# A two-layer hybrid decoder trunk with a dense and a fetched path for its experts: 40 tokens instead of 32 on the fetched path, and expert activations rounded in pairs

## The reference

```
q  = h @ wq                                  # 8 heads x 256
s1, s2 = q[:half] @ k1, q[half:] @ k2        # 128 scores each
top 16 of each, top 16 of their 256 sums     # 8 x 16 = 128 picks for each token
gates = softmax(top scores)
act = gelu(sum_d h[t, d] * u[expert, d])     # one number for each pick
y[t] = sum_k act[t, k] * gate[t, k] * v[expert, :]
```

## Time and profile before

| | |
|---|---|
| median of 3 runs | 2004.48 us |
| span of the profiled execution, first to last instruction | 2001.2 us |
| PE busy | 1945.8 us, 97% |
| DVE busy | 1710.9 us, 85% |
| ACT busy | 1240.9 us, 62% |
| POOL busy | 441.9 us, 22% |
| DMA, mean over the span | 240 GB/s |

### The profile page before, as it was taken

The page is one execution under the profiler, slowest core; times in us unless marked ns, Lnnn a source line. Parts: engine busy times, 40 slices in busy tenths (PEclk is TensorE's granted clock), DMA queues, the critical chain, the costliest instruction groups (busy, mean ns, idle before and its releaser), DMA issues.

```text
span 2001.2 us, 39536 instructions
## 1 busy us (share of the span) xinstructions
PE 1945.8 (97%) x14478; PEld 1854.1 (93%) x14478; DVE 1710.9 (85%) x3168; ACT 1240.9 (62%) x2387; POOL 441.9 (22%) x312
## 2 busy tenths in 40 slices
PE   6999999999999999999989998999999999999998
PEld 6899899999999999999978898999999999999997
DVE  7876988999799888888788878899988888888887
ACT  3478545666888655555555775566668885555554
POOL 0000000000556433344100000000016543443440
PEclk7999999999999999999999999999999999999999
DMA  8764755666666799988767557555665558999884
GB/s 334 276 238 149 262 191 171 200 199 203 212 214 208 251 319 324 321 322 322 257 229 249 206 173 248 197 190 197 200 210 169 165 163 289 323 319 321 323 321 139
DMA packets 133554, 480.52 MB, mean 240 GB/s; under 512 B 16048, under 2 KB 16688, under 8 KB 132784
## 3 DMA queue, kind: packets, MB, share of 16 engines
q1 hardware_dynamic: 114992, 411.74, 60.6%
q0 software_dynamic: 18432, 67.12, 8.9%
HBM read 473.61 MB, written 1.57 MB: 237 GB/s over the span
## 4 chain that ended last, share of the span: by engine, by line
PE 87%; DVE 6%; ACT 3%; issue 2%; DMA 2%; SPq 0%; POOL 0%; DVEq 0%; ACTq 0%
PE ps L1777 20%; PE ps L1773 12%; PE ps L1474 11%; PE ps L1416 9%; PE ps L1412 8%; PE ps L1413 8%; PE ps L1478 6%; PE ps L1409 2%; PE ps L1746 2%; PE ps L1518 2%; ACT w_hi L564 2%; DVE w_lo L865 1%; DMA raw<-in_win 1%; PE ps L1464 1%; PE ps L1705 1%
## 5 line engine op out<-in xcount | busy, mean ns | idle before, releaser
L865 DVE TENSOR_TENSOR w_lo<-raw,w_hi 128x1024 fp32r<-128x1024 f32 x664 | 812.0, 1223 | 164.3 <-ACT w_hi L564 161.6
L564 ACT CAST w_hi<-raw 128x1024 fp32r<-128x1024 f32 x664 | 695.1, 1047 | 395.7 <-PE ps L1416 204.5
L1777 PE MATMUL ps<-p_both,w_hi 128*128 128x448 f32 x1952 | 440.1, 367 | 1.0 <-DVE p_both L1255 1.0
L1412 PE MATMUL ps<-h_both,w_hi 128*128 128x224 f32 (+1 forms) x1640 | 393.9, 282 | 2.5 <-ACT big L569 1.2
L1413 PE MATMUL ps<-h_both,w_hi 128*128 128x224 f32 (+1 forms) x1640 | 386.4, 278 | 0.0
L1777 PEld LDWEIGHTS ps<-p_both,w_hi 128*128 128x128 f32 x1952 | 349.3, 189 | 24.5 <-issue 1.3
L540 POOL TENSOR_SCALAR hot<-con,rt 128x128 f32<-128x128 f32 x168 | 198.1, 1190 | 640.0 <-DVE neg L1330 528.4
L1412 PEld LDWEIGHTS ps<-h_both,w_hi 128*128 128x128 f32 x1640 | 314.1, 192 | 5.5 <-issue 3.3
L1413 PEld LDWEIGHTS ps<-h_both,w_hi 128*128 128x128 f32 x1640 | 314.6, 192 | 0.0
L792 ACT CAST p_both<-big 128x224 fp32r (+1 forms) x256 | 97.0, 380 | 303.5 <-PE ps L1773 303.5
L1773 PEld LDWEIGHTS ps<-p_both,w_lo 128*128 128x128 f32 x2048 | 269.2, 191 | 7.6
(11 more groups left out here) (214 smaller groups left out, 2363.9 us busy)
## 6 DMA issues: line engine op xcount, KB each, us to landing
raw<-in_u SPq DMA_DIRECT2D x256, 512.0 KB, 3.5
raw<-in_v SPq DMA_DIRECT2D x256, 512.0 KB, 5.5
raw<-in_win SPq DMA_DIRECT2D x104, 512.0 KB, 4.4
hot<-in_ada SPq DMA_DIRECT2D x60, 512.0 KB, 4.9
big<-in_ada SPq DMA_DIRECT2D x36, 512.0 KB, 6.3
raw<-in_wq SPq DMA_DIRECT2D x32, 512.0 KB, 4.6
raw<-in_wout SPq DMA_DIRECT2D x16, 512.0 KB, 4.0
big<-in_decay SPq DMA_DIRECT2D x2, 1536.0 KB, 12.6
```

The costliest lines, as they stand in the source:

```text
L564: nc.scalar.copy(w_hi[:, j % 2, :], raw[:, j, :]).then_inc(hi_ready, 1)
L865: tt(w_lo[:, j % 2, :], raw[:, j, :], w_hi[:, j % 2, :].bitcast(F32), ALU.subtract).then_inc(lo_ready, 1)
L1412: mm(o, w, h_hi[:, k, 0:nd], start=(k == 0), stop=False)
L1777: return mm(bank(YC[c])[:, 0:2 * nd].rearrange("p (a t) -> p a t", a=2), w_hi[:, s, P * c:P * (c + 1)], p_both[:, s, :, 0:nd], start=begin ...
```

## The change

It sends 40 instead of 32 tokens through the fetched path and 216 instead of 224 through the dense one.

- `DENSE` falls to 216: matmuls of 448 columns get 432, those of 224 get 216. `N_GATE` falls from 28 to 27.
- `SP_GROUPS` is 3, on 120 partitions (`SP_ROWS`). `SP_STEPS` rises from 32 to 43, since 128 picks in three groups take 43 steps; the 129th pick has a weight of zero. There are 86 indirect DMAs of 120 rows for each layer instead of 64 of 128 rows. `dot_at` and `mix_at` spread 43 steps over the same 57 blocks. Since 86 is no multiple of four, slot numbers run on from layer to layer.
- The token rows of the last 40 tokens are copied by three DMAs from a buffer of their own (`h_own`), and three DMAs of 40 rows spread the picks instead of four of 32. ACT and DVE write the upper 64 partitions (`TAIL`) where they wrote 32.
- Activations are rounded two blocks at a time: one ACT copy of 2 x 216 and one DVE subtraction of 2 x 216 for blocks m and m+1. Two pair slots are needed; the second lies in `h_both`, which is free in the V stage. ACT's copy for blocks m+2 and m+3 waits for block m-1 instead of block m, and DVE's subtraction now stands behind the `w_lo` of block m+1 instead of ahead of it. PE waits for it at even blocks only.
- POOL's one-hot loop goes by single builds instead of pairs, as 27 is odd.

The diff, cut to its core:

```diff
-N_SPARSE = 32
+N_SPARSE = 40
...
-SP_STEPS = N_PICK // SP_GROUPS
+SP_STEPS = -(-N_PICK // SP_GROUPS)
+SP_PICKS = SP_GROUPS * SP_STEPS
+SP_ROWS = SP_GROUPS * N_SPARSE
+TAIL = slice(P // 2, P)
...
-        mixed = words(0, D)
-        h_tok = words(W_SCORE, D)
+        mixed = words(0, D)[0:SP_ROWS]
+        h_tok = words(W_SCORE, D)[0:SP_ROWS]
+        h_own = words(W_SCORE + 3 * D, D)
...
-                        for g in range(SP_GROUPS - 1):
-                            sp.dma_start(h_tok[N_SPARSE * g:N_SPARSE * (g + 1), :], h_tok[P - N_SPARSE:P, :]).then_inc(tok_spread, 16)
+                        for g in range(SP_GROUPS):
+                            sp.dma_start(h_tok[N_SPARSE * g:N_SPARSE * (g + 1), :], h_own[P - N_SPARSE:P, :]).then_inc(tok_spread, 16)
...
+                    slot = (2 * SP_STEPS * l + j) % SP_SLOTS
...
-                        rows_in[j % SP_SLOTS], None, u_flat if j < SP_STEPS else v_flat,
-                        bass.IndirectOffsetOnAxis(spread[:, 0, k:k + 1].bitcast(U32), 0)).then_inc(row_in[j % SP_SLOTS], 16)
+                        rows_in[slot], None, u_flat if j < SP_STEPS else v_flat,
+                        bass.IndirectOffsetOnAxis(spread[:, 0, k:k + 1].bitcast(U32), 0)).then_inc(row_in[slot], 16)
...
-                def round_p(m, s):
...
-                    nc.scalar.copy(p_hi[:, s, 0:nd], acts[:, ds(m, 1), 0:nd].rearrange("p a t -> p (a t)")
-                                   ).then_inc(phi_ready, 1)
+                def round_pair(m, s):
...
+                    nc.scalar.copy(pair_hi[s][:, 0:2, 0:nd], acts[:, ds(m, 2), 0:nd]).then_inc(phi_ready, 1)
...
-                        for s in range(2):
-                            round_p(s, s)
+                        round_pair(0, 0)
...
-                        if not (end and j >= 2):
-                            act.wait_ge(block_done, n + 1)
-                            round_p(m + 2, j % 2)
+                        if j % 2 == 0 and not (end and j):
+                            act.wait_ge(block_done, n)
+                            round_pair(m + 2, 1 - j // 2)
...
-                def low_p(m, s):
...
-                    dve.wait_ge(phi_ready, l * N_V + m + 1)
-                    tt(p_lo[:, s, 0:nd], acts[:, ds(m, 1), 0:nd].rearrange("p a t -> p (a t)"),
-                       p_hi[:, s, 0:nd].bitcast(F32), ALU.subtract).then_inc(plo_ready, 1)
+                def low_pair(m):
...
+                    s = m // 2 % 2
+                    dve.wait_ge(phi_ready, (l * N_V + m) // 2 + 1)
+                    tt(pair_lo[s][:, 0:2, 0:nd], acts[:, m:m + 2, 0:nd], pair_hi[s][:, 0:2, 0:nd].bitcast(F32), ALU.subtract
+                       ).then_inc(plo_ready, 1)
...
-                    dve.wait_ge(row_in[n % SP_SLOTS], 16 * (2 * SP_STEPS // SP_SLOTS * l + n // SP_SLOTS + 1))
-                    return rows_in[n % SP_SLOTS]
+                    slot, turn = (2 * SP_STEPS * l + n) % SP_SLOTS, (2 * SP_STEPS * l + n) // SP_SLOTS
+                    dve.wait_ge(row_in[slot], 16 * (turn + 1))
+                    return rows_in[slot]
...
-                        dve.wait_ge(tok_spread, 16 * (SP_GROUPS - 1) * (l + 1))
+                        dve.wait_ge(tok_spread, 16 * SP_GROUPS * (l + 1))
...
-                low_p(0, 0)
+                low_pair(0)
...
-                            low_p(RING * i + j + 1, (j + 1) % 2)
-                        if not (end and j == RING - 1):
...
+                        if j % 2 == 0 and not (end and j):
+                            low_pair(RING * i + j + 2)
...
-                def part_y(s, c, which):
-                    pp, vv = ((p_hi, w_hi), (p_lo, w_hi), (p_hi, w_lo))[which]
-                    return mm(bank(YC[c])[:, 0:nd], vv[:, s, P * c:P * (c + 1)], pp[:, s, 0:nd],
+                def part_y(j, c, which):
+                    pp, vv = ((pair_hi, w_hi), (pair_lo, w_hi), (pair_hi, w_lo))[which]
+                    return mm(bank(YC[c])[:, 0:nd], vv[:, j % 2, P * c:P * (c + 1)], pp[j // 2][:, j % 2, 0:nd],
...
-                def both_y(s, c, begin):
-                    return mm(bank(YC[c])[:, 0:2 * nd].rearrange("p (a t) -> p a t", a=2), w_hi[:, s, P * c:P * (c + 1)],
-                              p_both[:, s, :, 0:nd], start=begin, stop=False, skip_group_check=True)
+                def both_y(j, c, begin):
+                    return mm(bank(YC[c])[:, 0:2 * nd].rearrange("p (a t) -> p a t", a=2), w_hi[:, j % 2, P * c:P * (c + 1)],
+                              (h_both[:, :, j - 2, 0:nd] if j >= 2 else p_both[:, j, :, 0:nd]), start=begin, stop=False, skip_group_check=True)
...
-                        s = j % 2
...
-                        pe.wait_ge(plo_ready, l * N_V + m + 1)
+                        if j % 2 == 0:
+                            pe.wait_ge(plo_ready, l * (N_V // 2) + i * (RING // 2) + j // 2 + 1)
```

More of the change, by code:

```diff
@@ L242, in build @@
         p_hi, p_lo = p_both[:, :, 0], p_both[:, :, 1]
+        pair_hi, pair_lo = (p_hi, h_hi), (p_lo, h_lo)
         cond = sb("cond", [P, D])
@@ L261, in build @@
         cond_t = sb("cond_t", [P, KC])
-        spare = sb("spare", [P, 2 * N_PICK + 3 * SP_STEPS])
+        spare = sb("spare", [P, 2 * SP_PICKS + 3 * SP_STEPS])
         number16 = sb("number16", [P, TOPK], F16)
@@ L270, in build @@
         sel = con[:, K_SEL:K_SEL + N_SPARSE]
-        picked = spare[:, 0:2 * N_PICK].rearrange("p (a k) -> p a k", a=2)
-        spread = spare[:, 2 * N_PICK:2 * N_PICK + 2 * SP_STEPS].rearrange("p (a k) -> p a k", a=2)
-        dots = spare[:, 2 * N_PICK + 2 * SP_STEPS:]
+        picked = spare[:, 0:2 * SP_PICKS].rearrange("p (a k) -> p a k", a=2)
+        spread = spare[0:SP_ROWS, 2 * SP_PICKS:2 * SP_PICKS + 2 * SP_STEPS].rearrange("p (a k) -> p a k", a=2)
+        dots = spare[0:SP_ROWS, 2 * SP_PICKS + 2 * SP_STEPS:]
         def words(at, *shape):
@@ L308, in build @@
         acts = words(0, NKEYS, DENSE)
-        mixed = words(0, D)
-        h_tok = words(W_SCORE, D)
+        mixed = words(0, D)[0:SP_ROWS]
+        h_tok = words(W_SCORE, D)[0:SP_ROWS]
+        h_own = words(W_SCORE + 3 * D, D)
         mod_ring2 = words(W_SCORE + D, 2, D)
-        rows_in = [t[:].rearrange("p s b n -> p (s b n)")[:, D * a:D * (a + 1)] for t in (hot1, hot2) for a in range(2)]
+        rows_in = [t[:].rearrange("p s b n -> p (s b n)")[0:SP_ROWS, D * a:D * (a + 1)] for t in (hot1, hot2) for a in range(2)]
         u_flat = u_rows
@@ L531, in _, with hot @@
                 pool.wait_ge(gates_ready, l + 1)
-                def hot(i, first=False):
-                    for s in range(2):
[L535 to L544, removed]
+                def hot(b):
+                    if b >= 2:
+                        pool.wait_ge(gate_mat, N_GATE * l + b - 1)
+                    for t in range(POOL_TOK):
+                        col = ds(b * BATCH + t, 1)
+                        last = nc.gpsimd.tensor_scalar(hot2[:, b % 2, t, :], iota, rt[:, 1, col], rt[:, 2, col],
+                                                       ALU.is_equal, ALU.mult)
+                    last.then_inc(hot2_pool, 1)
+                for b in range(N_GATE):
+                    hot(b)
                 pool.wait_ge(picks_spread, 16 * SP_GROUPS * (l + 1))
@@ L829, in _ @@
                             act.wait_ge(score_used, l + 1)
-                        nc.scalar.copy(h_tok[P - N_SPARSE:P, 512 * half:512 * (half + 1)], bank(M[half])[P - N_SPARSE:P]).then_inc(tok_copied, 1)
+                        nc.scalar.copy(h_own[TAIL, 512 * half:512 * (half + 1)], bank(M[half])[TAIL]).then_inc(tok_copied, 1)
                     if 8 <= m < 8 + 4 * n_fill and m % 4 == 0:
@@ L901, in angle @@
                     dve.wait_ge(angles, 2 * a + 2)
+            nc.vector.memset(picked[TAIL, :, N_PICK:], 0.0)
             dve.wait_ge(sig_c, 1)
@@ L1250, in product @@
                     tt(acts[:, m, 0:nd], acts[:, m, 0:nd], acted[:, m % 2, 0:nd], ALU.mult).then_inc(producted, 1)
-                def low_p(m, s):
-                    dve.wait_ge(phi_ready, l * N_V + m + 1)
-                    tt(p_lo[:, s, 0:nd], acts[:, ds(m, 1), 0:nd].rearrange("p a t -> p (a t)"),
-                       p_hi[:, s, 0:nd].bitcast(F32), ALU.subtract).then_inc(plo_ready, 1)
+                def low_pair(m):
[3 more added lines that the diff above has]
+                       ).then_inc(plo_ready, 1)
                 def stage_picks():
-                    tail = slice(P - N_SPARSE, P)
-                    a1, a2, g = (res[tail, a, PH:2 * PH, :].rearrange("p h k -> p (h k)") for a in range(3))
-                    number, weight = picked[tail, 0, :], picked[tail, 1, :]
+                    a1, a2, g = (res[TAIL, a, PH:2 * PH, :].rearrange("p h k -> p (h k)") for a in range(3))
+                    number, weight = picked[TAIL, 0, 0:N_PICK], picked[TAIL, 1, 0:N_PICK]
                     us.done(stt(number, a2, float(NKEYS), a1, ALU.mult, ALU.add))
@@ L1795, in outputs_y @@
                                     if c not in held:
```

(13 more changed lines are left out.)

## The result

The changed kernel takes 2176.25 us (median of 5 runs, 2164.67 to 2180.98) against 2004.48 us (2002.85 to 2007.14): 1.085 times as long, 95% interval 1.083 to 1.087. The forecast was 1992, with a range of its own of 1984 to 1998. All of the loss arises in the two V stages: from ACT's copy of the last block of `u` to that of the last block of `v` it was 326.7 us in either layer, and it is 414.5 and 403.9 now.

What follows compares the result with a forecast made beforehand. PE, busy 97% of the span, was taken as the bound. Terms - 12.1 - 1.8 - 2.0 + 0.4 + 3.0 = - 12.5 us took the span from 2001.2 to 1988.7; plus 3.3 gave 1992.0 us, own range 1984 to 1998.

Steps and rivals of the forecast that it cites:

- Transfers, V stage: V stage: DMAs can supply 360 GB/s, loads landing in about 6.5 us; 3 us lost over both layers.
- The first rival: V stage: loads landing over about 7.5 us let the four-slot ring set the pace; 2023 us at 8 us; chance 0.21.
- the 3 us put down for late loads: V stage: some loads of over 8 us that PE feels, 3 us lost over both layers.
- Wide matmuls: V stage: 432 instead of 448 columns saves 6.2 ns in each of 1952 matmuls, 12.1 us (11.3 to 13.1).
- Narrow matmuls: Matmuls of 224 columns already lie on an f32 weight-load floor near 110 ns; 216 columns save nothing.
- Rounding in pairs: ACT's part off the path; DVE's first subtraction of each V stage 0.22 us longer, 0.4 us lost over both layers.
- the 0.4 of the sum: Start of the V stages: PE waits longer for DVE's first subtraction, 0.4 us lost over both layers (0 to 1).
- Wide matmuls, U stage: U stage: DVE's `w_lo` sets the pace from near block 29; PE gains 0.9 us a layer, 1.8 in all (0 to 6.4).
- Gate builds: One gate build fewer for each layer shortens PE's list by 0.98 us, 2.0 us in all (1.8 to 3.5).

Runs made afterwards that it cites:

- the nine phases without computation: Fetches and/or 512 KB weight loads only, all layer computation left out; beside loads, fetches of 128 rows moved 408 GB/s and of 120 rows 273.
- full fetches: Changed kernel, but each fetch fills all 128 partitions, rows 120 to 127 fetching unread row 0: 1985.53 us; repeated later, 1983.14 us.

## Why the prediction was wrong

By its own steps:

**Transfers, V stage: this step failed.** It said that the DMAs can do it, because they had moved 426 GB/s with four fetches queued. That row was of fetches of 128 rows; the change fetches 120. I counted the smaller fetch as 6% less traffic, and it lowers what all 16 DMA engines deliver, the untouched weight loads included, in the nine phases without computation from 408 to 273 GB/s, in the kernel to 266. The demand of 360 GB/s was then 30% too much. For 128 rows the step holds: with full fetches the same window moved 363 GB/s. The two pages of the Trainium skill named above describe ports and dealing; I had read "120 rows" as a size and not as a shape.

**The first rival had the right path and the wrong cause.** It said that late loads let the ring set the pace, (landing + 1.05 + 1.23 + 0.2) / 4 for a block. With the 10.9 us measured that is 3.35 us; blocks 2 to 61 of layer 0 took 192.3 / 59 = 3.26. The 2023 us of this rival are 153 us short of what came. But I let it begin from traffic and stop at a landing of 8 us, and gave it 0.21. With full fetches, where its conditions were met as I had meant them (12% more traffic, DVE at 94% of the window), it didn't occur: ACT waited for loads for 15.6 us in 12 blocks of layer 0 and PE 0.2 us for a `w_lo`. So the 3 us put down for late loads measure 0.4 over both layers when the fetches are full; DVE held, as forecast.

```profile
ACT w_hi L570 <- DMA raw<-in_v: 15.6, 12, 1.5
...
PE ps L1780 <- DVE w_lo L869: 0.2, 1, 0.2
```

**Wide matmuls: right, undersized.** 448 to 432 columns was to save 6.2 ns of 204. In the chain of the V stage with full fetches eight take 1.57 us, 196 ns, and eight narrow ones 0.88:

```profile
882.15 1.57 PE ps L1784 x8
883.72 0.88 PE ps L1780 x8
884.60 1.56 PE ps L1784 x8
```

That is 8 to 9 ns each, more than the 6.7 of 16 columns at 2.4 GHz, 16 to 17 us in all instead of 12.1. The slope between 448 and 512 columns wasn't the slope below 448.

**Narrow matmuls: right.** Still 0.88 / 8 = 110 ns; 216 columns gain nothing. The page is read too narrowly in the prediction: the section that it cites of the Trainium skill ("TensorE: Matmul & The Clock Gate", Back-to-back issue gap) gives N / 2.4 + 2.5 ns for an isolated matmul, and says that in a stream of weight loads and matmuls both set the spacing. This kernel is such a stream, so the 111 ns don't contradict it.

**Rounding in pairs: right.** PE's waits for the first subtraction of a V stage rose from 1.0 to 1.4 us over both layers, the 0.4 of the sum.

**Wide matmuls, U stage: right.** For block 60 of layer 0 `w_lo` ends at 466.67 + 1.21 = 467.88 and PE's narrow part starts at 467.93, a lead of 0.05 us where it was 0.79. First DVE, then PE of the changed kernel:

```profile
466.67 1.21 DVE L867 TENSOR_TENSOR w_lo<-raw,w_hi 128x1024 fp32r<-128x1024 f32 x1
...
467.93 1.15 PE L1482 MATMUL ps<-h_both,w_lo 128*128 128x216 f32 x8
```

The lead reached this 0.05 us at block 29, the block that the prediction named, and from there two of every five blocks have no more (it said every fifth). Up to block 30 the stage was 1.5 us shorter than before; up to block 71 it is 0.8 us shorter in layer 0 and 1.1 in layer 1, for 0.9 forecast, since DVE sets the pace in between.

**Gate builds: right in sign, the size uncertain.** Blocks 71 to 127 of layer 1 take 180.5 to 180.6 instead of 181.0 us, those of layer 0 between 1.9 and 0.2 us less in the four profiles with 27 builds. Over both layers that is 0.7 to 2.3 us, where 2.0 was forecast (1.8 to 3.5).

**What the forecast would have been without the failed step.** For the version with full fetches, the last one profiled, the distances between ACT's copies of the same weight blocks in the two traces give:

```
us, both layers       before   pairs, full fetches   change   forecast
U stage, 0 to 127      750.5         747.0            -3.5      -3.8
V stage, to 127        653.3         637.2           -16.1      -8.7
```

The V row runs from the last block of U to the last of V. Its forecast is -12.1 + 0.4 + 3.0: its two errors, 4 to 5 us too little for the matmuls and 3 us for late loads that didn't show, have the same sign. With full fetches the kernel measured 1985.53 and 1983.14 us, 6 and 9 us under the forecast of 1992, the second just below its range.

## What to carry to other kernels

A DMA's destination is a shape and not a number of bytes: before giving up partitions of a transfer, measure it alone with the new number of rows, and keep the full 128 with dummy rows if it slows. Read the share of the DMA engines together with their rate; a share near 1 at a falling rate says that packets have become slower, not that there are more of them. And a capacity read from a row holds for transfers of the form in that row only.

## What the runs showed of the hardware that I had not expected

- Transfers of 120, 112 or 96 partitions into the SBUF move 236, 267 and 259 GB/s when fetched alone (plain loads 227 and 241, 305 and 268), where 128 partitions move 327 when fetched alone and 371 to 375 when loaded, and 408 with two queues.
- They slow the transfers of another queue as well: loads of 128 rows beside fetches of 120 rows share 273 GB/s, beside fetches of 128 rows 408.
- Two queues that write 64 partitions each, one to either half, move 237 GB/s, little more than the 206 to the same half; this is no substitute for one transfer of 128.
- Taking 16 columns from a matmul of 448 gained 8 to 9 ns, more than 16 cycles of the 2.4 GHz clock. I have no cause for it.
